# Moving the down-weight casts, the w_out buffers and the first FFN loads of an encoder block

## The reference, cut to what matters

```python
qa, ka, va, qb, kb, vb, ga, gb = split(x @ w_in)
out_a = gqa(rope(rms_norm(qa)) * scale, rope(rms_norm(ka)), va)   # 8 heads, 4096 keys
out_b = dilated_window_attention(qb * scale, kb, vb)              # 3 groups x 4 heads, 129 keys per query
gate_a = sigmoid(ga + b_gate[0]);  gate_b = sigmoid(gb + b_gate[1])
mixed = (gate_a * (out_a @ w_proj_a) + gate_b * (out_b @ w_proj_b)) @ w_out
x = layer_norm(ALPHA * x + mixed, ln1_g, ln1_b)
h = silu(x @ w_ffn_gate) * (x @ w_ffn_up)                         # 5632 hidden
x = layer_norm(ALPHA * x + h @ w_ffn_down, ln2_g, ln2_b)
```

## Time and profile before

| | |
|---|---|
| device time, median of the runs | 4113.2 us (lowest 4110.9) |
| the profiled execution | 4118.86 us; span of its slowest core (core 5) 4117.1 us |
| spans of its 8 cores | 4085.1 to 4117.1 us |
| PE busy on core 5 | 4006.5 us, 97% of the span |
| DVE, ACT, POOL busy | 31%, 25%, 11% |
| granted TensorE clock, mean of core 5 | 0.990 of full speed |

### The profile page before, as it was taken

How to read it: one execution, slowest core, us unless ns; L and a number is a source line. 1 busy time by engine, 2 the same in 40 slices (tenths; PEclk the granted TensorE clock), 3 DMA queues, 4 the chain that set the end, 5 groups by cost and what they waited for, 6 DMA issues and landing times.

```text
span 4117.1 us, 51864 instructions; the slowest of 8 cores (4085.1 to 4117.1 us)
## 1 busy us (share of the span) xinstructions
PE 4006.5 (97%) x19504; PEld 1865.7 (45%) x19504; DVE 1292.4 (31%) x1907; ACT 1033.4 (25%) x1257; POOL 460.5 (11%) x441
## 2 busy tenths in 40 slices
PE   7999999999998999999999999999999999999998
PEld 4644444444444544444444444444444444444443
DVE  3564444444444652222265210011101111011104
ACT  1235555555554541111132100001100111001100
POOL 3320000000000110101033100000100110000102
PEclk9999999999999999999999999999999999999999
DMA  9656575757655865645555754555546464655652
GB/s 155 127 86 95 88 99 86 108 85 99 118 108 115 223 163 92 106 82 93 173 187 182 245 171 138 192 167 202 180 139 199 154 204 133 205 174 160 204 186 84
DMA packets 209251, 597.88 MB, mean 145 GB/s; under 512 B 55216, under 2 KB 75184, under 8 KB 200624
## 3 DMA queue, kind: packets, MB, share of 16 engines
q1 hardware_dynamic: 171024, 451.88, 34.4%
q0 software_dynamic: 37984, 142.69, 24.5%
HBM read 662.78 MB, written 151.98 MB: 198 GB/s over the span
## 4 chain that ended last, share of the span: by engine, by line
PE 91%; DMA 5%; DVE 1%; ACT 1%; issue 1%; POOL 0%; SPq 0%; DVEq 0%; POOLq 0%; ACTq 0%
PE pbig L159 91%; DMA z_s<-ZS_141 2%; DMA X_59<-xT 1%; DMA WO_167<-wo_s 0%; PE pbig L157 0%; DMA kb_s<-KS_111 0%; DMA WG_184<-wfg_s 0%; DMA WD_193<-wfd_s 0%; DMA WD_191<-wfd_s 0%; DMA WKV_75<-wkv 0%; ACT PT_102 L173 0%; ACT PT_101 L173 0%; POOL YY_133_175 L179 0%; DVE AC_105 L179 0%; POOL YY_174 L179 0%
## 5 line engine op out<-in xcount | busy, mean ns | idle before, releaser
L173 ACT ACTIVATE SGL_203<-pbig 128x512 f32<-128x512 f32 x88 | 52.5, 597 | 924.0 <-PE pbig L159 923.8
L179 DVE TENSOR_TENSOR HT_190<-SGL_204,pbig 128x512 bf16<-128x512 f32 x88 | 60.5, 688 | 536.1 <-PE pbig L159 536.1
L173 ACT ACTIVATE PT_102<-pbig 128x1024 bf16<-128x1024 f32 x171 | 174.8, 1022 | 155.8 <-DVE AC_104 L179 52.4
L173 ACT ACTIVATE PT_101<-pbig 128x1024 bf16<-128x1024 f32 x171 | 174.7, 1022 | 145.0 <-PE pbig L159 49.8
L173 ACT ACTIVATE PT_103<-pbig 128x1024 bf16<-128x1024 f32 x170 | 173.8, 1022 | 143.6 <-PE pbig L159 50.2
L179 DVE TENSOR_TENSOR HT_190<-SGL_203,pbig 128x512 bf16<-128x512 f32 x88 | 60.5, 688 | 470.1 <-PE pbig L159 464.9
L159 PE MATMUL pbig<-WD_191,HT_190 128*128 128x512 bf16 x832 | 194.1, 379 | 1.8 <-DMA WD_191<-wfd_s 1.2
L159 PE MATMUL pbig<-WD_193,HT_190 128*128 128x512 bf16 x816 | 190.3, 379 | 2.5 <-DMA WD_193<-wfd_s 2.3
L159 PE MATMUL pbig<-WD_192,HT_190 128*128 128x512 bf16 x816 | 189.2, 379 | 1.0 <-DMA WD_192<-wfd_s 0.5
L173 ACT ACTIVATE SGL_204<-pbig 128x512 f32<-128x512 f32 x88 | 52.5, 597 | 508.3 <-PE pbig L159 508.3
L191 DVE SCALAR_TENSOR_TENSOR YY_152_194<-XR_156_198,pbig 128x512 f32<-128x512 f32 x16 | 11.0, 688 | 508.8 <-PE pbig L159 508.8
(11 more groups left out here) (775 smaller groups left out, 7157.7 us busy)
## 6 DMA issues: line engine op xcount, KB each, us to landing
WG_184<-wfg_s SPq DMA_DIRECT2D x60, 512.0 KB, 4.9
WU_187<-wfu_s SPq DMA_DIRECT2D x60, 512.0 KB, 6.2
WG_185<-wfg_s SPq DMA_DIRECT2D x58, 512.0 KB, 5.4
WU_188<-wfu_s SPq DMA_DIRECT2D x58, 512.0 KB, 6.7
WG_186<-wfg_s SPq DMA_DIRECT2D x58, 512.0 KB, 5.0
WU_189<-wfu_s SPq DMA_DIRECT2D x58, 512.0 KB, 6.2
WD_191<-wfd_s SPq DMA_DIRECT2D x52, 512.0 KB, 3.7
WD_192<-wfd_s SPq DMA_DIRECT2D x51, 512.0 KB, 3.7
```

Of the source, the lines that this page charges most:

```text
L173: return self.add("act", lambda e: e.activation(out=out, in_=in_, func=func, **kw), ins, [out])
L179: return self.add(eng, lambda e: e.tensor_tensor(out=out, in0=a, in1=b, op=op), [a, b], [out])
```

## The change: what it does

Three edits.

**Casts.** Attention B issues no piece of `wfd_s` any more. The merge issues pieces one at a time, each behind the gate-B sigmoid of a token block, 23 in all; the first FFN block issues the other 21, one behind each step's second SiLU.

**Placement of w_out.** `WO[0]` goes to 98 KiB (over the first half of `QA`), `WO[1..3]` to 2, 18 and 34 (over `X[0..2]`). `XR` goes to 114 and 122, `YY` to 50 and 58 (over `X[3]`). In the last chunk of the merge SP issues `WO[0]` first, ahead of the gate-B matmuls; `XR[0]` and `XR[1]` follow one by one.

**End of the w_out stage and start of the FFN.** Tiles 14 and 15 take the column blocks in the order 1, 2, 3, 0. `X1T[0]` is issued ahead of the last transposes of that stage (tile 11) and of the store behind them, and the first two `WG`, `WU` pairs behind blocks 2 and 3. The third pair, whose buffers now lie where `YY` is, is issued in step 1 of the FFN, behind the casts of tiles 14 and 15, which move from steps 2 and 3 to step 1.

```diff
@@ attention B
-        if t < NQ:
-            precast_to(NPRE + int((t + 1) * 12 / NQ), ex)
@@ merge
-    WO = [at("WO", 2 + 16 * fb, [128, 16, 512], BF16) for fb in range(4)]
+    WO = [at("WO", (98, 2, 18, 34)[fb], [128, 16, 512], BF16) for fb in range(4)]
-    XR = [at("XR", 98 + 8 * i, [128, D], F32) for i in range(2)]
-    YY = [at("YY", 114 + 8 * i, [128, D], F32) for i in range(2)]
+    XR = [at("XR", 114 + 8 * i, [128, D], F32) for i in range(2)]
+    YY = [at("YY", 50 + 8 * i, [128, D], F32) for i in range(2)]
...
         if k == 15:
-            for i in range(2):
-                s.dma("sp", XR[i][:, :], xs_d[i * 128:(i + 1) * 128, :])
+            wo_load(0)
+            s.dma("sp", XR[0][:, :], xs_d[0:128, :])
...
-            s.actf(SB[:, :], b, AF.Sigmoid, bias=bgate[:, 16 + f:17 + f], scale=1.0)
+            sg = s.actf(SB[:, :], b, AF.Sigmoid, bias=bgate[:, 16 + f:17 + f], scale=1.0)
+            precast_to(NPRE + (k * 4 + tb + 1) * 22 // 60, sg)
...
-            if k == 15:
-                wo_load(tb)
+            if k == 15 and tb < 3:
+                wo_load(tb + 1)
+                if tb == 0:
+                    s.dma("sp", XR[1][:, :], xs_d[128:256, :])
...
-        precast_to(NPRE + 12 + int((k + 1) * (len(pre) - NPRE - 12) / 16), sg)
@@ w_out stage, tiles 14 and 15
-    for fb in range(4):
+    for n, fb in enumerate((1, 2, 3, 0)):
...
-        if fb == 0:
-            p6_tr(11, (2, 6, 3, 7))
+        if n == 0:
             load_x1T(0)
-        else:
-            ensure_gu(fb)
+            p6_tr(11, (3, 7, 0, 4))
+        elif n < 3:
+            ensure_gu(n)
@@ FFN
-            ensure_gu(min(gi + 3, (tb + 1) * 22))
-            if tb == 0 and j in (2, 3):
-                p6_cast(12 + j)
+            if gi == 1:
+                p6_cast(14)
+                p6_cast(15)
+            ensure_gu(min(gi + 3, (tb + 1) * 22) if gi else 2)
...
-                s.actf(sg[:, :], pg, AF.Silu)
+                sl = s.actf(sg[:, :], pg, AF.Silu)
...
+            if tb == 0:
+                precast_to(NPRE + 22 + j + 1, sl)
```

## The result

The changed kernel takes 4073.95 and 4072.91 us in two runs; the kernel before takes 4113.2 us in the median of its three runs beside them (4110.9 to 4114.5). The ratio is 0.9904 with a 95% interval of 0.9875 to 0.9933, some 39.5 us less. In a second session of runs the ratio was 0.9895, interval 0.9841 to 0.9948. Runs in which a die was granted a lower clock, such as two more of the changed kernel, 4361.69 and 4405.39 us at about 0.92, are left out of every comparison of whole times. The forecast was 4087, from a sum of -28.4 us; the measured time is inside the range and inside the 2%, but the change won 11 us more than the sum, and 4073 lies nearer to the second rival's 4066 than to the forecast.

A forecast was written before the change was run, and what follows sets the result against it. PE, busy 97%, was taken as the bound, so only its standing or low-clock time could be won. -15.7 - 7.3 - 6.9 + 1.5 = -28.4 us gave 4090.5 (profiled) or 4084.8 (median); forecast 4087, range 4064 to 4106.

The forecast's parts named there:

- second rival: Attention B and FFN start: casts were all of the loss; attention B wins 34.2 us, total 4066; chance 0.14.
- Term 1: Attention B: fewer late z stores without casts; 13.8 us of idle and 1.9 for one restart, -15.7 us.
- three long stands: Attention B: PE waits of 9.9, 7.1 and 8.4 us behind late z stores, each with 3.3 us taken off.
- the bounds, 3 to 34.2: Attention B's gain: 3 us if stores are late for another reason, 34.2 if each cast costs nearer 8.6 than 3.3.
- my own sign, idle below 5 us: Attention B: PE idle below 5 us would show the forecast wrong and point to the second rival.
- First rival: Attention B: z stores wait in their own queue, not for casts; wins 3 instead of 15.7, total 4100; chance 0.20.
- Term 2: First w_out block: issued earlier, so PE's 5.4 us wait for WO_167 and a 1.9 us restart go, -7.3 us.
- the order cannot fall behind: w_out blocks: each later one is wanted 6.9 us after the one before and issued 4.3 us after it.
- Term 3: FFN start: X1T issued earlier, WG_184 only 1.5 us late; 5.0 us and a 1.9 us restart won, -6.9 us.
- Term 4: Third weight pair, FFN: waits for casts and stores of tiles 14 and 15, so arrives late, +1.5 us.
- At nothing: Merge's 23 casts, first FFN block's 21, block order and places cost nothing; an FFN step needs 9.9 of 13.8 us.
- slower rival: First FFN block: casts starve the weight loads, at most 29 us more, total 4116, or 4188 at 12 us each; chance 0.06.

The follow-up runs named there:

- e1: Kernel before with the cast edits alone (none in attention B, 23 in merge, 21 in first FFN block); 0.9915 of before, attention B 190.2 us.
- e2: Changed kernel with its cast edits undone (12 casts in attention B, 32 in merge); 0.9984 of before, attention B 217.3 us.
- e3: Changed kernel with 24 casts in attention B instead of none; attention B 261.0 us against 190.0.
- e4: Changed kernel with 6 casts in attention B instead of none; attention B 195.0 us against 190.0.
- e5: Kernel before with four z buffers instead of two for the first 28 of 36 z tiles; attention B 202.8 us against 216.1.
- e11: Kernel before with the moved casts and X1T's load issued ahead of the last transposes' store; w_out stage 244.6 us.
- e7: Changed kernel with the 21 casts of the first FFN block doubled; that block's gate/up 385.2 us against 309.9.
- e12: Changed kernel with 7 further casts in the first FFN block; that block's gate/up 326.0 us against 309.9.

## Why the prediction was right, and where it was wrong

**Term 1, attention B (-15.7): the mechanism held, the size did not; this step failed.** The casts do hold back the z stores (e1), and the price of a cast was about right: 3.3 us of the engines in the sum (from a queue of which about half was gate weights), 3.1 to 3.7 by the queues. What was wrong was how often it counts. I took it off once for each of the three long stands, for the one cast issued in the flight of the late store, and left 14.7 us standing. Between the profiled cores some 24 us of standing went and 7 us of matmuls at the low clock, where I had 13.8 and 1.9. By the series of e2, e3 and e4 the 7.5 casts above the first four or five cost 7.5 x 3.64 = 27.3 us. That a cast pushes back not only the store beside it but what comes behind as well is my reading of this; no run isolates it, and e5 shows that about half of the loss needed the short reach of two buffers too. Of the bounds, 3 to 34.2, the upper was the near one (31.7 between the profiled cores). By my own sign, idle below 5 us, the second rival described attention B; its total of 4066 was 7 us too low, because its other terms were too large, and the forecast 14 us too high.

**First rival: refuted.** With the loads in place (e1) ZS costs 2.4 us on the profiled core and 3.5 in the mean of the cores, where it cost 20.6. The Trainium skill's page "DMA: Bandwidth & Descriptors", section "Queues, rings and completion order", says that an engine takes the descriptors of one queue in ring order; I drew from it that only a part would come back. Only the store of 1306.23, 15.39 us, is still late behind the loads, and there POOL's transfers are in flight as well. The measured stage decides, and it came back nearly whole.

**Term 2, first w_out block (-7.3): right in kind, a little less.** The wait is gone, and the merge is 5.5 us shorter between the profiled cores, 4.4 in the mean. But it needed no new place: the casts alone removed the long wait (e1), as the order alone did (e2), and the prediction had named the two casts there only in passing. And "the order cannot fall behind" was wrong: it compared when blocks are issued with when they are wanted, and left out what else is in the row. With the residual and a cast among them the blocks come at 248 GB/s where PE takes 304. That gave back 2.1 us at WO_169.

**Term 3, start of the FFN (-6.9): the wait went as forecast, a part of the gain was given back.** WG_184 was 0.2 us late where I took 1.5, for the reason given (e11 isolates it). But the w_out stage won 3.4 us in the mean, 4.1 between the profiled cores: 6.3 less for WG_184 and 1.2 by the clock, less the 2.1 of WO_169 and 1.3 of XTS_181 (tile 13's store beside X1T). Another 1.3 for SGL_203 (ACT behind LayerNorm 1) falls into the next stage. The prediction follows ACT only 20 us into the FFN, where nothing happened, and not at its first SiLU.

**Term 4, third pair (+1.5): right in size, on another path.** WG_186 went out at 2233.32, as its buffer lies over tile 14's `YY` alone; only WU_189 waited for tile 15's store. It then took 12.1 us to land, not 5.0, and was 1.5 us late. Two other cores wait 1.2 and 2.3 us for it, five do not.

**At nothing: the casts in the FFN held, with less room than I said.** They cost at most 1.2 us. I had 9.9 of 13.8 us per step, which leaves room for a second cast; e7 shows that there is none, and e12 that there is not even room for one more in every third step. The step's loads are not the weights alone: SP moved 46.54 MB in 260 us, 2.5 MB per step, at 61.7% x 260 / 46.54 = 3.4 us per MB, so 8.5 us and 3.1 for the cast, 11.6 of 13.8. The slower rival's mechanism is real and was less than one more cast per step away. In e7 loads on SP's queue land 30 us after issue in place of 5.0, because of casts from POOL's. This agrees with what the Trainium skill's page "DMA: Bandwidth & Descriptors" says in its section "Issuing engines are not separate DMA queues". PE's standing grows by about the same per cast in both stages: 3.0 us from e2 to e3 in attention B, (63.3 - 2.2) / 21 = 2.9 us in e7.

So the forecast was right by its range, and that in part by luck: two errors went against each other. Between the profiled cores term 1 was short by 31.7 - 15.7 = 16.0 us, and terms 2 to 4 had 12.7 where 5.5 + 4.1 - 1.5 = 8.1 came.

## What to carry to other kernels

Price a background transfer by the engine time of all 16 DMA engines, but do not count it only beside a visible wait: in attention B nearly every cast beyond the first few cost about that much. Two experiments tell what it costs. Halve and double the number, and read the threshold and the slope; and give the waiting side more buffers, to see how much of the cost is their short reach. For loads in a row, compare the rate at which the whole row is delivered, with everything that stands in it, with the rate at which the loads are used, not the times of issue.

## What the runs showed of the hardware that was not expected

- Free DMA time in a stage's mean says little. After the change the queues of attention B leave 100 - 70.7 = 29% of 190 us, 55 us, free; twelve casts at 3.6 us are 43, and still they cost the stage 26 us. Nearly half of the free part lies in the stage's last quarter (0.39 busy, first quarter 0.87), and with four buffers instead of two the same twelve cost 18.6.
- The same 512 KB load of gate weights lands 5.0 us after issue without casts, 11 to 13 with a cast per step, and 30 with two, while PE's waits for the weights of the block behind the first are none, 1.5 and 67 us: the landing time rises before PE waits.
- A 1 MB store with 2 MB issued 0.4 us behind it landed in 4.4 to 5.9 us over the eight cores, without them in 3.9 to 4.7.
